# A two-layer decoder step: group weights ahead of the query, a split combination, and the sample projection in column groups

## What is computed

```python
def combine_groups(outs, lses):                      # layer 1, three groups
    o = jnp.stack(outs, axis=2).astype(jnp.float32)
    w = jax.nn.softmax(jnp.stack(lses, axis=2), axis=2)
    return jnp.sum(o * w[..., None], axis=2).astype(outs[0].dtype)

def dil_layer(...):
    ...
    dil_out = dil_fn(qd).reshape(b, t, D_DIL) * jax.nn.silu(gd)
    q = rms_norm(mq.reshape(b, t, MEM_HEADS, HEAD_DIM), mem_q_g) * (HEAD_DIM ** -0.5)
    mem_out = mem_attend(q, mem_kv).reshape(b, t, D_MEM) * jax.nn.silu(mg)
    out = jnp.concatenate([dil_out, mem_out], axis=-1) @ w_out
    return x + out
```

## Time and profile before

| | us |
|---|---|
| median of 3 runs | 2722.89 (2721.72 to 2724.37) |
| the profiled execution | 2719.55, its span 2717.4 |
| TensorE busy in the span | 2702.2 (99%) |
| VectorE busy | 1789.1 (66%) |
| ScalarE busy | 1112.9 (41%) |

### The profile page before, as it was taken

One profiled execution on the slowest core, in us unless ns is written; L12 is line 12 of the kernel. 1 busy time (PEld: TensorE's weight loads), 2 busy tenths in 40 slices (PEclk: granted clock), 3 DMA queues, 4 the chain that ended last, 5 costly groups with the idle time before them and its releaser, 6 DMA issues.

```text
span 2717.4 us, 41295 instructions
## 1 busy us (share of the span) xinstructions
PE 2702.2 (99%) x14834; PEld 2259.7 (83%) x14834; DVE 1789.1 (66%) x3925; ACT 1112.9 (41%) x3346; POOL 383.1 (14%) x610
## 2 busy tenths in 40 slices
PE   9999999999999999999999999999999999999999
PEld 7788888888887888878888888888888889998887
DVE  7686766768678644435575667877674767777764
ACT  7533131212326234225434353532332349876632
POOL 0101010100101000000112032333424223210000
PEclk9999999999999999999999999999999999999999
DMA  8486555655676734324266676787768789757642
GB/s 281 143 250 208 183 167 179 207 182 171 210 246 207 222 115 156 101 97 152 94 246 228 211 268 216 274 284 264 247 237 284 262 311 330 231 177 262 217 154 82
DMA packets 292628, 567.75 MB, mean 209 GB/s; under 512 B 32432, under 2 KB 91760, under 8 KB 292424
## 3 DMA queue, kind: packets, MB, share of 16 engines
q1 hardware_dynamic: 257032, 462.31, 52.0%
q0 software_dynamic: 35392, 102.80, 10.6%
HBM read 432.28 MB, written 132.72 MB: 208 GB/s over the span
## 4 chain that ended last, share of the span: by engine, by line
PE 93%; DVE 4%; DMA 1%; ACT 1%; issue 1%; SPq 0%; DVEq 0%; ACTq 0%
PE ps L130 27%; PE ps L132 26%; PE ps L131 26%; PE ps L4133 2%; PE ps L3736 2%; PE ps L1385 1%; PE ps L4142 1%; PE ps L3774 1%; PE ps L3719 1%; PE ps L3035 1%; PE ps L3040 1%; PE ps L228 1%; PE ps L3130 1%; DMA a_raws<-w_mem_dram 0%; DVE a_wp L124 0%
## 5 line engine op out<-in xcount | busy, mean ns | idle before, releaser
L130 PE MATMUL ps<-b_wp,b_sring 128*128 128x512 f32 x640 | 250.5, 391 | 0.0
L131 PE MATMUL ps<-b_wp,b_sring 128*128 128x512 f32 x640 | 249.2, 389 | 0.0
L132 PE MATMUL ps<-b_wp,b_sring 128*128 128x512 f32 x640 | 249.1, 389 | 0.0
L130 PE MATMUL ps<-a_sring,a_wp 128*128 128x512 f32 x512 | 200.0, 391 | 0.0
L131 PE MATMUL ps<-a_sring,a_wp 128*128 128x512 f32 x512 | 199.3, 389 | 0.0
L132 PE MATMUL ps<-a_sring,a_wp 128*128 128x512 f32 x512 | 199.2, 389 | 0.0
L130 PE MATMUL ps<-b_wp,b_xthi 128*128 128x512 f32 x480 | 188.3, 392 | 0.0
L131 PE MATMUL ps<-b_wp,b_xthi 128*128 128x512 f32 x480 | 187.0, 389 | 0.0
L132 PE MATMUL ps<-b_wp,b_xtlo 128*128 128x512 f32 x480 | 186.7, 389 | 0.0
L1200 DVE TENSOR_TENSOR shared_o<-ps,b_spare 128x512 f32<-128x512 f32 x160 | 109.7, 685 | 112.3 <-PE ps L132 97.1
L1032 ACT ACTIVATE ps<-shared_o 128x128 f32<-128x128 f32 x390 | 103.4, 265 | 163.2 <-DVE shared_o L1200 146.0
(11 more groups left out here) (494 smaller groups left out, 6877.3 us busy)
## 6 DMA issues: line engine op xcount, KB each, us to landing
b_sring<-sums_dram SPq DMA_DIRECT2D x160, 512.0 KB, 5.2
a_sring<-sums_a_dram SPq DMA_DIRECT2D x128, 512.0 KB, 5.1
b_raws<-w_b_dram SPq DMA_DIRECT2D x176, 256.0 KB, 4.5
a_raws<-w_a_dram SPq DMA_DIRECT2D x140, 256.0 KB, 4.1
kv_dram<-shared_o POOLq DMA_DIRECT2D x96, 256.0 KB, 4.0
tok_b_dram<-shared_o POOLq DMA_DIRECT2D x96, 256.0 KB, 4.3
front<-tok_b_dram SPq DMA_DIRECT2D x96, 256.0 KB, 3.9
front<-grp_dram SPq DMA_DIRECT2D x48, 260.0 KB, 4.2
```

The lines of the kernel that those rows point to most:

```text
L130: pe.matmul(acc, a_hi, b_hi, start=first, stop=False)
L131: pe.matmul(acc, a_hi, b_lo, start=False, stop=False)
L132: return pe.matmul(acc, a_lo, b_hi, start=False, stop=last)
```

## The change

1. In layer 1, from step 2 on, `weights(t)` follows `joint_max(t)` on VectorE and `weighted_sum(t)` follows `group_weights(t)` on ScalarE, both ahead of the query. The four heads' exponentials are no longer parted.
2. `combine` takes the groups as an argument: group 1 is added after `gate(t-1)`, ahead of `maxima(t)`; group 2 and the product with the gate stay after `low_o(t-1)`.
3. TensorE turns the mix ahead of the probabilities, from step 2 on.
4. The sample projection of both layers takes whole rows: `cat` is no longer split, each chunk of the weights is multiplied in four matmuls of 128 columns, one a head, whose outputs lie 32 partitions apart. The zeroing of `cat`, the low parts, the copy of the low sums and their semaphores go; `add` has four additions of 128 columns a half. The second half now waits for `y_added`, the last of these.

The diff, cut to its core (renamed semaphores and removed helpers are left out):

```diff
-        self.cat = core.sb(st, f"{tag}_cat", [P, self.KO, LOW + S], F32R)
+        self.cat = core.sb(st, f"{tag}_cat", [P, self.KO, LOW + S])
...
+    def projected_at(self, h):
+
+        return self.bank(slice(h * LOW, h * LOW + S), slice(0, HD))
...
     def project(self, pe, half):
         if half:
-            pe.wait_ge(self.y_begun, 1)
+            pe.wait_ge(self.y_added, 1)
         else:
-            pe.wait_ge(self.og_lo, 1)
+            pe.wait_ge(self.og_copied, 1)
         for k in range(self.KO):
-            w_hi, w_lo = self.operands.wo(k, half)
-            acc = self.bank(slice(0, LOW + S), slice(0, C))
-            pe.matmul(acc, self.cat[:, k, :], w_hi, start=(k == 0), stop=False)
-            m = pe.matmul(acc, self.cat[:, k, :], w_lo, start=False, stop=(k == self.KO - 1))
+            for part, w in enumerate(self.operands.wo(k, half)):
+                for h in range(H):
+                    m = pe.matmul(self.projected_at(h), self.cat[:, k, 0:S], w.bitcast(F32)[:, h * HD:(h + 1) * HD],
+                                  start=(k == 0 and part == 0), stop=(k == self.KO - 1 and part == 1))
         m.then_inc(self.projected, 1)
...
     def setup(self, dve):
-        dve.memset(self.cat.bitcast(F32)[:, :, :], 0.0).then_inc(self.zeroed, 1)
         dve.memset(self.sel[:, :], 0.0).then_inc(self.zeroed, 1)
...
     def add(self, dve, half):
         dve.wait_ge(self.projected, half + 1)
-        dve.wait_ge(self.low_copied, half + 1)
         dve.wait_ge(self.xs_in, 16)
-        xs = self.xs[:, half, :]
-        dve.tensor_tensor(xs, self.bank(slice(0, S), slice(0, C)), xs, ALU.add).then_inc(self.y_begun, 1)
-        dve.wait_ge(self.y_begun, half + 1)
-        dve.tensor_tensor(xs, self.low, xs, ALU.add).then_inc(self.y_added, 1)
+        for h in range(H):
+            xs = self.xs[:, half, h * HD:(h + 1) * HD]
+            m = dve.tensor_tensor(xs, self.projected_at(h), xs, ALU.add)
+        m.then_inc(self.y_added, 1)
...
                 if not conv and t > 1:
                     group_weights(t)
+                    weighted_sum(t)
                 if conv or t > 1:
                     query_high(t)
...
                 act.wait_ge(biased, t + 1)
-                exponentials(t, (0, 1))
-                if not conv and t > 1:
-                    weighted_sum(t)
-                exponentials(t, (2, 3)).then_inc(exped, 1)
+                exponentials(t, range(H)).then_inc(exped, 1)
...
-            def combine(t):
+            def combine(t, groups):
                 u = t % 2
                 dve.wait_ge(od_begun, t + 1)
-                for g in (1, 2):
+                for g in groups:
...
-                dve.tensor_tensor(od[:, :], od[:, :], gd_b[:, u, :], ALU.mult).then_inc(ops, 1)
+                if 2 in groups:
+                    dve.tensor_tensor(od[:, :], od[:, :], gd_b[:, u, :], ALU.mult).then_inc(ops, 1)
...
                 if not conv and t > 1:
                     joint_max(t)
+                    weights(t)
                 if t > (UNITS_UNTIL if conv else 1):
                     query_low(t)
                 if not (conv and t <= UNITS_UNTIL):
                     gate(t - 1)
+                if not conv and t > 1:
+                    combine(t, (1,))
                 if t >= 2:
                     add_right(t - 2)
...
                 maxima(t)
...
-                if not conv and t > 1:
-                    weights(t)
                 if conv or t > 1:
                     low_o(t - 1)
                 if conv:
                     mix_low(t)
                 else:
-                    combine(t)
+                    combine(t, (2,) if t > 1 else (1, 2))
...
                 dec_middle(t)
+                if not conv and t > 1:
+                    turn_mix(t)
                 turn_probs(t)
-                if not conv:
+                if not conv and t == 1:
                     turn_mix(t)
```

More of the change, by code:

```diff
@@ L2606, in open @@
             self.keys.open(st, {"mem": self.ring}, {"mem": [self.qb[:, n, :] for n in range(2)]})
-            self.low = core.sb(st, f"{tag}_low", [S, C])[:, :]
+            core.sb(st, f"{tag}_low", [S, C])
         else:
@@ L2612, in open @@
             self.xs = spare0[0:S, 6:8, C:2 * C]
-            self.low = spare1[0:S, 6, C:2 * C]
             self.qn, self.kn, self.vn = (core.sb(st, f"{tag}_{n}", [HS, 3, HD]) for n in ("qn", "kn", "vn"))
@@ L2622, in open @@
             self.outputs(st)
-        self.cat = core.sb(st, f"{tag}_cat", [P, self.KO, LOW + S], F32R)
+        self.cat = core.sb(st, f"{tag}_cat", [P, self.KO, LOW + S])
         self.sel = core.sb(st, f"{tag}_sel", [P, S * S])
         names = ("v_in0 v_in1 v_in2 v_in3 rows_in gates_in xs_in zeroed sel_made weighed joined gathered "
-                 "rows_turned rows_hi rows_lo s_turned maxed biased exped inverted scaled "
-                 "p_turned p_copied gated og_turned og_hi og_lo projected low_copied y_begun y_added y_out")
+                 "rows_turned rows_copied s_turned maxed biased exped inverted scaled "
+                 "p_turned p_copied gated og_turned og_copied projected y_added y_out")
         self.sems = sems = core.sems(st, tag, names)
         (self.rows_came, self.gates_in, self.xs_in, self.zeroed, self.sel_made, self.weighed, self.joined,
-         self.gathered, self.rows_turned, self.rows_hi, self.rows_lo, self.s_turned,
+         self.gathered, self.rows_turned, self.rows_copied, self.s_turned,
          self.maxed, self.biased, self.exped, self.inverted, self.scaled, self.p_turned, self.p_copied,
-         self.gated, self.og_turned, self.og_hi, self.og_lo, self.projected, self.low_copied, self.y_begun,
-         self.y_added, self.y_out) = sems[4:]
+         self.gated, self.og_turned, self.og_copied, self.projected, self.y_added, self.y_out) = sems[4:]
         self.v_in = sems[0:4]
@@ L2732, in gather @@
             if self.conv:
-                pe.wait_ge(self.rows_lo, 1)
+                pe.wait_ge(self.rows_copied, 1)
         elif b == 0:
@@ L2762, in project, with copy_rows @@
         if half:
[L2763 removed]
+            pe.wait_ge(self.y_added, 1)
         else:
[L2765 removed]
+            pe.wait_ge(self.og_copied, 1)
         for k in range(self.KO):
[L2767 to L2770 removed]
+            for part, w in enumerate(self.operands.wo(k, half)):
+                for h in range(H):
+                    m = pe.matmul(self.projected_at(h), self.cat[:, k, 0:S], w.bitcast(F32)[:, h * HD:(h + 1) * HD],
+                                  start=(k == 0 and part == 0), stop=(k == self.KO - 1 and part == 1))
         m.then_inc(self.projected, 1)
[L2774 to L2775 removed]
+    def copy_rows(self, act):
         act.wait_ge(self.rows_turned, 1)
         act.activation(self.cat[:, 0:KD, 0:S], self.bank(slice(0, P), slice(0, KD * S)).rearrange(
[L2778 removed]
+            "p (k s) -> p k s", s=S), ACT.Copy).then_inc(self.rows_copied, 1)
     def width(self, kind):
@@ L2806, in og_cols, with copy_og @@
         return slice(self.KO - len(self.kinds) * H, self.KO), slice(0, len(self.kinds) * H * S)
-    def og_high(self, act):
+    def copy_og(self, act):
         chunks, cols = self.og_cols()
-        act.wait_ge(self.zeroed, 2)
         act.wait_ge(self.og_turned, 1)
         act.activation(self.cat[:, chunks, 0:S], self.bank(slice(0, P), cols).rearrange("p (k s) -> p k s", s=S),
[L2813 to L2819, removed]
+                       ACT.Copy).then_inc(self.og_copied, 1)
     def setup(self, dve):
-        dve.memset(self.cat.bitcast(F32)[:, :, :], 0.0).then_inc(self.zeroed, 1)
         dve.memset(self.sel[:, :], 0.0).then_inc(self.zeroed, 1)
-        dve.wait_ge(self.zeroed, 2)
+        dve.wait_ge(self.zeroed, 1)
         dve.memset(self.sel[:, 0:S * S:S + 1], 1.0).then_inc(self.sel_made, 1)
[L2828 to L2831, removed]
     def new_products(self, dve):
@@ L3373, in dec_begin @@
                 if conv and t == 1:
-                    dec.rows_high(act)
+                    dec.copy_rows(act)
                 if t == SOFT0:
@@ L3383, in dec_begin @@
                 if t == GATED + 1:
-                    dec.og_high(act)
-                if t == GATED + 2:
-                    dec.copy_low(act, 0)
-                if t == GATED + 3:
-                    dec.copy_low(act, 1)
+                    dec.copy_og(act)
             def weighted_sum(t):
@@ L3584, in dec_end @@
                     dec.new_values(dve)
-                if conv and t == 1:
-                    dec.rows_low(dve)
                 if conv and t < UNITS_UNTIL:
```

8 lines of the change are left out of this document (removed).

## The result

The changed kernel takes 2731.53 us (median of six runs, 2730.83 to 2733.69); the kernel before, on the same chip, takes 2721.82 us (six runs, 2720.86 to 2724.37). The ratio is 1.0033 with an interval of 1.0022 to 1.0043: slower, by 9.7 us. A second comparison gave 2730.77 against 2722.78, 8.0 us and 1.0034 [1.0021, 1.0046]. The forecast was 2729.8 us, with a range of 2725.5 to 2735.

A forecast was written before the change was run, and what follows sets the result against it. TensorE, busy for all 17.00 us of a step, was taken as the bound. Terms 6.8 + 1.0 − 0.9 − 0.2 + 0.2 = 6.9 us on 2722.89 gave 2729.8 us, range 2725.5 to 2735.

The forecast's parts named there:

- Waits of scores, 6.8: Layer 1's output stage: scores waits for query_low in steps 2, 4 to 8 and 12, 6.8 us, bounds 5.8 to 7.8.
- J − Q: Start of joint_max on VectorE less start of turn_query on TensorE; scores waits J − Q + 0.80 where above zero.
- Hidden: Rival, chance 0.13: chain shorter or joint_max earlier, so scores doesn't wait; 2721.8 us, no change.
- the 0.86 it needed: How many us more step 6 needs for joint_max to precede turn_query by over 0.80, under rival Hidden.
- priced at 0.41 in other steps: turn_mix ahead of turn_probs: next joint_max 0.41 us later, added in steps 7, 8 and 12, not 4 to 6.
- low_o, 1.0: Output projection's second dozen waits for low_o: 0.1 us in seven steps, 0.3 in step 3; together 1.0, bounds 0 to 2.5.
- Turns, −0.9: Second half of combine ends earlier, removing turn_mix's small wait: 0.15 us in six steps, gain 0.9, bounds 0 and 1.2.
- The sample's projection and its adds, 0.0 together: Sample projection in column groups gains 0.2 us; layer 1's second half waits 0.2 for the four adds, bounds 0 and 0.7.
- the 0.5 at which I had said I would be wrong: Stated failure test: the two layers' sample projections move the time by more than 0.5 us.
- The sum, 6.9: Whole kernel: all terms together make it 6.9 us longer, taken as +4.5 to +9.5.
- More steps wait: Rival, chance 0.07: combine's first half delays low_o in 14 steps, some 0.5 us more each; 2733 to 2735 us.
- Column groups: Rival, chance 0.02: sample projection's 240 added matmuls cost 0.057 us each on top, 13.7 us; 2743 us.

The follow-up runs named there:

- the run with probabilities first: The changed kernel with turn_probs ahead of turn_mix again, the old order of the turns; 2729.07 us, ratio 1.0025, stage 281.02 us.
- the weights alone: The kernel before with only weights and weighted_sum moved ahead of the query; 2726.32 us, ratio 1.0014, stage 278.57 us.
- the weights between: The kernel before with only weights moved right behind query_low and weighted_sum right behind high_o; 2720.66 us, ratio 0.9996, stage 273.71 us.
- the first run: The kernel before with only the sample projection in column groups; 2723.78 us against 2722.06, ratio 1.0006, stage 275.62 us.

## Why the prediction came out as it did

The direction, the place and the main price were right. By its own terms:

- **Waits of scores, 6.8.** Measured 6.9, in the seven steps named, and per step 0.84, 0.84, 0.86, 0.86, 0.86, 1.91, 0.71 against the 0.78, 0.86 three times, 0.83, 1.91 and 0.69 forecast. The chain from joint_max to scores was put at 3.98 and is 4.01.
- **But steps 4 to 6 came out right for a wrong reason.** I took J − Q from the kernel before, 0.06, and said that the swapped turns leave these steps alone, because a slab ends about there anyway. Freed of weighted_sum, ScalarE ends the slab earlier: in the run with probabilities first J − Q is −0.31 in step 6 and the wait 0.49, and in the run with the weights alone it is 0.42 in steps 5 and 6 and 0.18 in step 4. That is the mechanism of the rival Hidden, worth some 0.4 us and not the 0.86 it needed. The swapped turns then took it back: the 0.37 above, for an order that I had priced at 0.41 in other steps and at nothing in these. In step 4 the split of combine takes it back by itself, the wait being 0.79 in the run with probabilities first. Two omissions cancelled to 0.0 a step, which was luck.
- **A term that was missing, 0.7.** The twelve matmuls of scores take about 0.1 us longer in each step in which they had to wait. In step 6 the first matmul after the wait has the next at a distance of 0.22, where 0.11 is usual:

```profile
2531.23 0.39 PE L130 MATMUL ps<-b_xtlo 128*128 128x256 f32 x1 [0.70 <-DVE b_xtlo L3575]
2531.45 0.28 PE L131 MATMUL ps<-b_xtlo 128*128 128x256 f32 x1
2531.57 0.28 PE L132 MATMUL ps<-b_xtlo 128*128 128x256 f32 x1
```

- **low_o, 1.0.** Measured 1.1: 0.40 in step 3 (0.3 forecast), the rest 0.05 to 0.14 in the steps that wait (0.1 forecast). The list of waits names only the one in step 3; the others are found on TensorE's weight loads. The row of step 6, and in the row below it the matmul that it loads for, which starts without idle time:

```profile
2535.96 0.19 PEld L130 LDWEIGHTS ps<-b_xthi,out_cathi 128*128 128x128 f32 x1 [0.26 <-DVE out_catlo L3525]
```

```profile
2535.96 0.50 PE L130 MATMUL ps<-b_xthi,out_cathi 128*128 128x512 f32 x1
```

- **Turns, −0.9.** Measured −1.36, and for another reason. I credited the split, by which the second half of combine ends earlier. With combine whole and the old order (the weights alone, the weights between) the gain is −1.36 in either. It comes from weights and weighted_sum being done early, wherever that is; neither the split nor the swap adds to it.
- **The sample's projection and its adds, 0.0 together.** Measured +0.57 in layer 1's stage and −0.1 in layer 0. In layer 0 a half takes 5.36 us from its first matmul to the next work (1165.87 to 1171.23), under the 5.45 to 5.55 I gave:

```profile
1165.56 0.39 PE L132 MATMUL ps<-a_xthi,out_cat 128*128 128x512 f32 x1
1165.87 0.41 PE L2771 MATMUL ps<-a_xthi,dec_cat 128*8 128x128 f32 x8
1166.10 0.40 PE L2771 MATMUL ps<-a_xtlo,dec_cat 128*8 128x128 f32 x8
1166.32 0.40 PE L2771 MATMUL ps<-a_xthi,dec_cat 128*8 128x128 f32 x8
...
1170.90 0.40 PE L2771 MATMUL ps<-a_xtlo,dec_cat 128*8 128x128 f32 x8
1171.23 0.66 PE L3691 MATMUL ps<-ident,out_q 128*128 128x128 f32 x4
1171.72 1.50 PE L3708 MATMUL ps<-a_spare 128*128 128x128 f32 x12
```

  A group of four takes 0.22 us. The way in is 0.31 and not 0.23, the way out 0.33 and the transposes behind it 0.49 and not 0.44 (1168.64 to 1169.08), so a half is 0.06 shorter in all. In layer 1, with 16 groups and not 24, the shorter groups don't make up for way in and out, some 0.1 a half. The second half waits for the four adds, as feared:

```profile
2686.73 1.17 DVE L2885 TENSOR_TENSOR b_spare<-ps,b_spare 8x128 f32<-8x128 f32 x4
```

```profile
2687.95 0.41 PE L2771 MATMUL ps<-b_xthi,dec_cat 128*8 128x128 f32 x8 [0.21 <-DVE b_spare L2885]
```

  I took 0.2 for that wait; by the distances of step 14 it is 0.3. The run with the projection alone, where the adds came in time, lost 0.33 in the stage. Where TensorEngine Tiling (Array Packing) of the Trainium skill, section Performance Considerations, counts some 60 cycles for each matmul and so an estimated 6.0 us here, the trace disagrees: 0.055 us a matmul, a quarter of 0.22, is all there is. The two layers together come to about +0.5, next to the 0.5 at which I had said I would be wrong; of the way in and out and of the wait for the adds I had put too little in the sum.
- **The sum, 6.9.** In the stage 7.9 by these terms (6.9 + 0.7 + 1.1 − 1.4 + 0.6) and 7.99 by its two ends. The mis-sized terms are the restart of scores (0.7) and the projection (0.6), against them the turns (−0.5). The second comparison measured 8.0 us, the first 9.7; the 1.7 between them lies inside the interval of either, and no row of the stage answers to it.

Of the rivals, More steps wait did not show: steps 9 to 11 and 13 to 15 kept their distances (0.0 from turn_query to scores). Hidden showed as a part, above. Column groups fell with the first run.

What stays open is why the stage starts anywhere from 2435.5 to 2439.6 us in three executions that share all the code ahead of it (2437.9 and 2440.4 in two of the changed kernel).

## What to carry to other kernels

On a kernel whose TensorE never idles, an operation moved ahead of a step that TensorE waits for is priced by start times, not by busy time: add up the chain across the engines, handovers included, and set it against the start of the covering work, step by step. Put early work behind what TensorE needs soonest from that engine, and where the engine has time left before the next such thing: here weights fitted between query_low and low_o on VectorE, and weighted_sum behind high_o on ScalarE, at no cost that the stage showed. When a reordering is credited with a gain, undo each piece by itself: here the gain in the turns came from one move, and two others that were meant to go with it cost 2.3 and 1.7 us.

## What the runs showed of the hardware

- In the seven steps that waited, a short wait cost TensorE more than its length: the first matmul of 256 columns after one kept the next away for 0.19 to 0.22 us and not 0.11.
- A wait of TensorE can stand on the weight load alone, 0.26 us in the row above, with no idle time on the matmul; the matmuls still lose about 0.1 by their distances.
- Four matmuls of whole rows with eight stationary columns, in four column groups, take 0.22 us for 128 columns each, as long as one rounded matmul of 512 columns (0.23); entering and leaving that form costs about 0.1 us each.
- After waits of about 2.2 us TensorE's granted clock fell to 0.50 in three steps of the kernel with the weighted sum done twice, and sixteen matmuls took 3.14 us where they take 1.88 at 1.00; other waits of that length left the clock at 1.00.
